# Block 2: v from stationary weights, then turned; pooled maps in attention steps 8 to 11; weight splits ahead of the sigmoids and by halves

## The reference, cut to what matters

```python
u = rms_norm_2(h, norm_mix[l])
proj = u @ w_in[l]
z_pool, q, k, v, g_pool, g_attn = jnp.split(proj, splits, axis=-1)
y_pool = multiscale_pool(z_pool, w_pool_group[l], pool_scale[l]) @ w_pool_branch[l]
y_attn = windowed_gqa(q, k, v, sink[l]) @ w_attn_branch[l]
merged = jax.nn.sigmoid(g_pool) * y_pool + jax.nn.sigmoid(g_attn) * y_attn
h = h + merged @ w_out[l]
u = rms_norm_2(h, norm_ffn[l])
h = h + (jax.nn.silu(u @ w_ffn_gate[l]) * (u @ w_ffn_up[l])) @ w_ffn_down[l]
```

## Time and profile before

| | us |
|---|---|
| median of 3 runs | 678.34 (677.67 to 678.72) |
| the profiled execution | 676.9 |
| span of its instructions | 675.1 |

### The profile page before, as it was taken

One profiled execution on the slowest core, in us unless ns is written; L12 is line 12 of the kernel. 1 busy time (PEld: TensorE's weight loads), 2 busy tenths in 40 slices (PEclk: granted clock), 3 DMA queues, 4 the chain that ended last, 5 costly groups with the idle time before them and its releaser, 6 DMA issues.

```text
span 675.1 us, 10135 instructions
## 1 busy us (share of the span) xinstructions
PE 628.7 (93%) x3987; PEld 470.5 (70%) x3987; DVE 359.2 (53%) x705; ACT 292.9 (43%) x553; POOL 49.4 (7%) x72
## 2 busy tenths in 40 slices
PE   8999999998998785879899999999999999999996
PEld 5979867743533230424389999898888888888884
DVE  5687765641031020110188977657866666666665
ACT  6855663321011010100185756655655555555554
POOL 2100102000010000000049000000100000000001
PEclk9999999999999977969999999999999999999998
DMA  8956429999999999999997334355545555555101
GB/s 340 419 237 250 179 105 405 371 399 425 426 386 426 420 420 423 419 421 422 422 420 276 132 125 148 106 185 188 186 164 190 201 190 192 187 187 187 63 1 62
DMA packets 26286, 180.73 MB, mean 268 GB/s; under 512 B 3184, under 2 KB 3312, under 8 KB 5120
## 3 DMA queue, kind: packets, MB, share of 16 engines
q1 hardware_dynamic: 25200, 177.60, 66.7%
q10 hardware_dynamic: 1040, 2.50, 1.0%
HBM read 179.04 MB, written 1.05 MB: 267 GB/s over the span
## 4 chain that ended last, share of the span: by engine, by line
PE 71%; DMA 14%; DVE 8%; ACT 4%; issue 2%; POOLq 0%; SPq 0%; POOL 0%; ACTq 0%; DVEq 0%
PE ps L1625 68%; DMA ring<-stream_dram 14%; PE ps L1628 3%; DVE ring_r L411 2%; ACT single L404 1%; DVE work L1560 1%; ACT work L900 1%; DVE work L1563 1%; DVE h L1613 0%; DVE work L1616 0%; ACT turned L905 0%; ACT work_r L896 0%; DVE extra_r L510 0%; DVE work L1441 0%; ACT work L810 0%
## 5 line engine op out<-in xcount | busy, mean ns | idle before, releaser
L1625 PE MATMUL ps<-turned,single 128*128 128x256 f32 (+2 forms) x944 | 231.5, 327 | 1.3 <-DVE turned L1578 0.6
L1625 PE MATMUL ps<-turned,ring_r 128*128 128x256 f32 (+1 forms) x648 | 179.7, 281 | 0.0
L1625 PEld LDWEIGHTS ps<-turned,single 128*128 128x128 f32 x944 | 156.4, 189 | 18.0 <-issue 2.0
L411 DVE TENSOR_TENSOR ring_r<-ring,single 128x1024 fp32r<-128x1024 f32 (+1 forms) x132 | 159.8, 1233 | 11.2 <-ACT single L404 11.0
L404 ACT ACTIVATE single<-ring 128x1024 fp32r<-128x1024 f32 (+1 forms) x132 | 134.1, 1047 | 0.1
L1625 PEld LDWEIGHTS ps<-turned,ring_r 128*128 128x128 f32 x648 | 121.1, 188 | 0.4
L1625 PE MATMUL ps<-ring,work 128*32 128x512 f32 (+2 forms) x462 | 71.0, 621 | 18.1 <-DMA ring<-stream_dram 15.8
L1625 PEld LDWEIGHTS ps<-single 128*128 128x128 f32 x257 | 38.3, 189 | 33.9 <-issue 20.5
L1625 PE MATMUL ps<-single,turned 128*128 128x512 f32 (+3 forms) x208 | 59.2, 364 | 1.6 <-DVE ring_r L411 0.9
L1625 PE MATMUL ps<-single 128*128 128x512 f32 (+1 forms) x257 | 55.3, 353 | 3.5 <-DVE single L1452 2.3
L1625 PE MATMUL ps<-single,work_r 128*128 128x512 f32 x176 | 56.2, 392 | 0.0
(11 more groups left out here) (260 smaller groups left out, 733.1 us busy)
## 6 DMA issues: line engine op xcount, KB each, us to landing
ring<-stream_dram SPq DMA_DIRECT2D x145, 1024.0 KB, 12.3
work<-stream_dram SPq DMA_DIRECT2D x12, 1024.0 KB, 11.4
turned_w<-stream_dram SPq DMA_DIRECT2D x4, 1024.0 KB, 14.0
extra<-stream_dram SPq DMA_DIRECT2D x2, 1024.0 KB, 12.0
ring<-stream_dram SPq DMA_DIRECT2D x2, 832.0 KB, 8.0
h<-x_dram SPq DMA_DIRECT2D x2, 512.0 KB, 5.0
gain<-gains_dram ACTq DMA_DIRECT2D x2, 512.0 KB, 11.0
yields<-stream_dram SPq DMA_DIRECT2D x1, 1024.0 KB, 12.4
```

Source lines behind the costliest of these rows:

```text
L411: dve.tensor_tensor(ring_r[:, place, a], ring[:, place, a], w_hi[k % HIGHS][:, a].bitcast(F32), ALU.subtract).then_inc(s["wlo_done"], 1)
L1625: return pe.matmul(o, lhsT, rhs, start=start, stop=stop, **kw)
```

## The change

- v becomes a chunk like the others (weights held, 256 tokens moving, into bank 1); ACT copies it to a spare buffer (`v2_turned`), and PE turns it back with two transposes in step 0, from where ACT scales it out as before, one step later. PE's 48 matmuls with 128 moving become 24 with 256 moving and two transposes.
- `values2` takes both token halves in one matmul: 4 matmuls with 256 moving (two runs of 128) instead of 8 with 128, and waits for all four turned probabilities at once.
- The pooled maps move into steps 8 to 11, one each, between scores and turning, into the free half of bank 4 or 5; ACT and DVE take them out in their loops. The turning of steps 10 to 13 waits for `yp_low` in addition.
- The branch phase no longer waits for `o2_low` at its start, but ahead of its second half of step 0.
- ACT's and DVE's splits move: slot 6 and 7 in the first steps; slot 15 ahead of the sigmoids; 16 to 20 one half for each step m.

```diff
+        def pool_map_place(c):
+            return ps[:, 4 + (POOL_MAPS_AT + c) % 2, TOK:2 * TOK]
...
+            act.wait_ge(s["v2_ps"], 1)
+            act.activation(v2_turned, ps[:, 1, 0:TOK], ACT.Copy).then_inc(s["v2_sb"], 1)
             def values_out():
-                act.wait_ge(s["v2_ps"], 1)
+                act.wait_ge(s["v2_ps"], 2)
...
+                if u == 2 * HEADS:
+                    split_high_half(act, SPLIT1 + 15, 0)
...
                 if u == 0:
+                    split_high(act, SPLIT1 + 6)
+                if u == 1:
                     values_out()
-                    split_high(act, SPLIT1 + 6)
-                if u < 2 * HEADS:
+                    split_high_half(act, SPLIT1 + 7, 0)
+                if POOL_MAPS_AT < u <= POOL_MAPS_AT + 4:
+                    pool_map_high(act, u - POOL_MAPS_AT - 1)
+                if 0 < u < 2 * HEADS:
                     split_high_half(act, SPLIT1 + 7 + u // 2, u % 2)
             attention2_out(act, CT - 1)
-            for m in range(4):
-                act.wait_ge(s["yp_ps"], m + 1)
-                act.activation(yp_hi[:, m, :], ps[:, (4, 5, 0, 1)[m], 0:TOK], ACT.Copy,
...
+            split_high_half(act, SPLIT1 + 15, 1)
             for m in range(DT):
                 act.wait_ge(s["g_sb"], m + 1)
                 act.activation(gate[:, m, :], gate[:, m, :], ACT.Sigmoid).then_inc(s["sig_done"], 1)
+            split_high_half(act, SPLIT1 + 16, 0)
             for m in range(DT):
-                if m % 2 == 0:
-                    split_high(act, SPLIT1 + 15 + m // 2)
                 act.wait_ge(s["mg_sum"], m + 1)
                 act.activation(mg_hi[:, m, :], gate[:, m, 0:TOK], ACT.Copy).then_inc(s["mg_high"], 1)
+                split_high_half(act, SPLIT1 + 16 + (m + 1) // 2, (m + 1) % 2)
...
-                if u:
+                if u == 2:
+                    split_low_half(dve, SPLIT1 + 7, 0)
+                if u > 1:
                     split_low_half(dve, SPLIT1 + 7 + (u - 1) // 2, (u - 1) % 2)
+                if POOL_MAPS_AT + 1 < u <= POOL_MAPS_AT + 5:
+                    pool_map_low(dve, u - POOL_MAPS_AT - 2)
...
+            split_low(dve, SPLIT1 + 15)
             for m in range(DT):
-                if m % 2 == 0:
-                    split_low(dve, SPLIT1 + 15 + m // 2)
...
+                split_low_half(dve, SPLIT1 + 16 + m // 2, m % 2)
                 dve.wait_ge(s["mg_high"], m + 1)
...
+            pe.wait_ge(s["z2_sb"], 3)
+            chunk(ps[:, 1, 0:TOK], SPLIT1 + 4, 1, (u_hi, u_lo)).then_inc(s["v2_ps"], 1)
...
+            def values_turned():
+                pe.wait_ge(s["v2_sb"], 1)
+                pe.wait_ge(s["q2_sb"], 3)
+                for i in range(NT):
+                    last = turn(ps[:, 6, i * P:(i + 1) * P], v2_turned[:, i * P:(i + 1) * P])
+                last.then_inc(s["v2_ps"], 1)
...
+                c = u - POOL_MAPS_AT
+                if 2 <= c < 6:
+                    pe.wait_ge(s["yp_low"], c - 1)
...
-            def values2(m, i):
+            def values2(m):
...
+                pe.wait_ge(s["pt2_sb"], 4 * (m + 1))
...
-                        last = mm(ps[j * HD:(j + 1) * HD, 6 + m % 2, i * P:(i + 1) * P], v2[:, k, kv * HD:(kv + 1) * HD],
+                        last = mm(ps[j * HD:(j + 1) * HD, 6 + m % 2, 0:TOK], v2[:, k, kv * HD:(kv + 1) * HD],
+                                  pt2[:, j:4:2, k * P:(k + 1) * P], k == 0, k == NT - 1, skip_group_check=True)
...
+                if POOL_MAPS_AT <= u < POOL_MAPS_AT + 4:
+                    c = u - POOL_MAPS_AT
+                    pe.wait_ge(s["dp_done"], c + 1)
+                    pe.wait_ge(s["pt2_sb"], u - 1)
+                    if c >= 2:
+                        pe.wait_ge(s["yp_low"], c - 1)
+                    mm(pool_map_place(c), vec[:, V_PG + c * P:V_PG + (c + 1) * P], dp[:, c, :], True, True
+                       ).then_inc(s["yp_ps"], 1)
+                if u == 0:
+                    values_turned()
...
             pe.wait_ge(s["yp_low"], 4)
-            pe.wait_ge(s["o2_low"], CT)
...
+                    if m == 0 and b:
+                        pe.wait_ge(s["o2_low"], CT)
```

More of the change, by code:

```diff
@@ L470, in attention2_out @@
         def attention2_out(act, hp):
-            act.wait_ge(s["o2_ps"], 2 * (hp + 1))
+            act.wait_ge(s["o2_ps"], hp + 1)
             act.activation(at_hi[:, hp, :], ps[:, 6 + hp % 2, 0:TOK], ACT.Copy).then_inc(s["o2_sb"], 1)
@@ L517, in gate_out, with pool_map_high, pool_map_low @@
                               row2.unsqueeze(1).to_broadcast([P, 2, TOK]), ALU.mult).then_inc(s["g_sb"], 1)
+        POOL_MAPS_AT = 8
+        def pool_map_place(c):
+            return ps[:, 4 + (POOL_MAPS_AT + c) % 2, TOK:2 * TOK]
+        def pool_map_high(act, c):
+            act.wait_ge(s["yp_ps"], c + 1)
+            act.activation(yp_hi[:, c, :], pool_map_place(c), ACT.Copy, scale=vec[:, V_PSC + c:V_PSC + c + 1]
+                           ).then_inc(s["yp_sb"], 1)
+        def pool_map_low(dve, c):
+            dve.wait_ge(s["yp_sb"], c + 1)
+            dve.scalar_tensor_tensor(yp_lo[:, c, :], pool_map_place(c), vec[:, V_PSC + c:V_PSC + c + 1],
+                                     yp_hi[:, c, :].bitcast(F32), ALU.mult, ALU.subtract).then_inc(s["yp_low"], 1)
         def turned_bank(t):
@@ L900, in _ @@
                 act.activation(gate[:, m, :], gate[:, m, :], ACT.Sigmoid).then_inc(s["sig_done"], 1)
+            split_high_half(act, SPLIT1 + 16, 0)
             for m in range(DT):
-                if m % 2 == 0:
-                    split_high(act, SPLIT1 + 15 + m // 2)
                 act.wait_ge(s["mg_sum"], m + 1)
                 act.activation(mg_hi[:, m, :], gate[:, m, 0:TOK], ACT.Copy).then_inc(s["mg_high"], 1)
-            for n in range(19, B2 + 2):
+                split_high_half(act, SPLIT1 + 16 + (m + 1) // 2, (m + 1) % 2)
+            split_high_half(act, SPLIT1 + 20, 1)
+            for n in range(21, B2 + 2):
                 split_high(act, SPLIT1 + n)
@@ L1567, in _ @@
                                   ).then_inc(s["mg_done"], 1)
-            for n in range(19, B2 + 2):
+            for n in range(20, B2 + 2):
                 split_low(dve, SPLIT1 + n)
@@ L2152, in _ @@
             chunk(ps[:, 0, 0:TOK], SPLIT1 + 4, 0, (u_hi, u_lo), frees=1).then_inc(s["k2_ps"], 1)
-            def values(i):
-                for t in range(DT):
-                    begin, last = triple(ps[:, 6, i * P:(i + 1) * P], [u[:, t, i * P:(i + 1) * P] for u in (u_hi, u_lo)],
-                                         [w[:, D + t * P:D + (t + 1) * P] for w in split_pair(SPLIT1 + 4)], t == 0, t == DT - 1)
-                return last
-            split_ready(SPLIT1 + 4, 1)
-            pe.wait_ge(s["q2_sb"], 3)
-            values(0)
+            pe.wait_ge(s["z2_sb"], 3)
[6 more added lines that the diff above has]
+                last.then_inc(s["v2_ps"], 1)
             def scores2(u):
@@ L2185, in turn_probs2 @@
                 last.then_inc(s["pt2_ps"], 1)
-            def values2(m, i):
-                u, kv = 4 * m + 2 * i, m // 2
-                pe.wait_ge(s["pt2_sb"], u + 2)
-                if u == 0:
-                    pe.wait_ge(s["v2_sb"], 1)
-                if m >= 2 and i == 0:
+            def values2(m):
+                kv = m // 2
+                pe.wait_ge(s["pt2_sb"], 4 * (m + 1))
+                if m == 0:
+                    pe.wait_ge(s["v2_sb"], 2)
+                if m >= 2:
                     pe.wait_ge(s["o2_low"], m - 1)
@@ L2196, in values2 @@
                     for j in range(2):
-                        last = mm(ps[j * HD:(j + 1) * HD, 6 + m % 2, i * P:(i + 1) * P], v2[:, k, kv * HD:(kv + 1) * HD],
-                                  pt2[:, 2 * i + j, k * P:(k + 1) * P], i == k == 0, i == 1 and k == NT - 1, skip_group_check=True)
+                        last = mm(ps[j * HD:(j + 1) * HD, 6 + m % 2, 0:TOK], v2[:, k, kv * HD:(kv + 1) * HD],
+                                  pt2[:, j:4:2, k * P:(k + 1) * P], k == 0, k == NT - 1, skip_group_check=True)
                 last.then_inc(s["o2_ps"], 1)
@@ L2204, in _ @@
             scores2(1)
-            values(1).then_inc(s["v2_ps"], 1)
             for u in range(2 * HEADS):
@@ L2214, in _ @@
                     scores2(u + 2)
+                if POOL_MAPS_AT <= u < POOL_MAPS_AT + 4:
[8 more added lines that the diff above has]
+                    values_turned()
                 if u and u % 4 == 0:
-                    values2(u // 4 - 1, 0)
-                    values2(u // 4 - 1, 1)
+                    values2(u // 4 - 1)
                 turn_probs2(u)
-            values2(CT - 1, 0)
-            values2(CT - 1, 1)
-            for c in range(4):
-                pe.wait_ge(s["dp_done"], c + 1)
-                if c == 2:
-                    pe.wait_ge(s["g_sb"], DT)
-                mm(ps[:, (4, 5, 0, 1)[c], 0:TOK], vec[:, V_PG + c * P:V_PG + (c + 1) * P], dp[:, c, :], True, True
```

(3 more changed lines are left out.)

7 lines of the change are left out of this document (1 added, 6 removed).

## The result

The changed kernel ran at a median of 674.61 us (674.12 to 674.76, four runs), the kernel before beside it at 678.53: a ratio of 0.9944 [0.9925, 0.9963], or 3.9 us. All three together, 26 runs of it against 77 of the kernel before, put the medians at 675.56 and 678.59 and the means at 675.98 and 678.51, so 2.5 to 3.0 us. Executions of one and the same kernel, before or after, differ by 4 us and more, and the experiments place nearly all of that difference ahead of the code that the change touches.

What follows compares the result with a forecast made beforehand. PE's matmuls were taken to bound the attention stretch; terms of -1.0 + 0 + 2.0 + 0.5 - 3.1 - 0.5 = -2.1 us, taken off the median of 678.34, gave 676.2 us, range 674.8 to 678.3.

Steps and rivals of the forecast that it cites:

- v: Start of the attention stretch: v made as a chunk saves 1.75 us, of which 1.0 us stays after step 2.
- the chain of distances: DVE's work up to step 2's probabilities, 7.41 us from 377.55, putting step 2's turning at 385.05 instead of 386.05.
- Values: Value matmuls in steps 4, 8, 12 and behind step 15: one wide matmul instead of two, no change in time.
- rival D: Value matmuls no longer run in pairs: 0.85 us more a call, 3.4 for four, total 679.6 us; chance 0.11.
- Last values: Behind step 15's turning: the last values now wait for all of ACT's copy, +0.5 us.
- The end: Between last values and branch: the 3.08 us of maps and waiting vanish, -3.1 us.
- the cover of 3 us behind the sigmoids: In the branch: DVE's second product is ready at 447.1, and PE asks for it at 450.1.
- The projection's wait: Output projection: PE's wait for a weight's low part before the matmul of 471.92 goes, -0.5 us.
- Rival E: The end is not freed, the branch waits for DVE behind the sigmoids: 678.3 us if it eats all; chance 0.04.
- maps: Steps 8 to 11: each pooled map adds 0.5 us to PE's loop, +2.0 us for four.
- Rival C: A map costs 0.7 instead of 0.5 us and DVE's chain in step 2 is 0.3 longer: 677.3 us; chance 0.20.

Runs made afterwards that it cites:

- splits back: The changed kernel with the branch's and projection's weight splits back in the old order; 141.43 us from the first block-2 matmuls to the feed-forward, in one execution.
- third profile of the changed kernel: The changed kernel measured once more with nothing changed; ratio 0.9952 to the kernel before, median 675.51 us, block 2 beginning at 344.53.

## Why the prediction was right, and where it was not

**What held.** PE's matmuls bound the stage, and the time came from where the prediction put it. v: -1.03 against -1.0, and for the reason given, PE standing at the turning of step 2 for DVE's low parts (0.47 us, where 0.6 was written, at 384.76, which is 385.02 on the clock of the kernel before; the chain of distances gave 385.05). Values: +0.04 against 0; the call takes 1.08 us against 1.09. The rule of the Trainium skill, "Advanced Engine Details and Errata", section "Memory Cachelines", that non-contiguous PSUM patterns slow matmuls, has no counterpart here on the reading side, and rival D with its 1.6 us a call falls by the same row. Last values: +0.53 against +0.5. The end: -3.19 against -3.1, and the cover of 3 us behind the sigmoids was there: the second product at 445.3 against a bound of 447.1. The projection's wait: -0.50 against -0.5 in this profile, -0.3 to -0.4 in the other two. Rival E, the branch waiting for DVE, did not happen, and would not have with the old order of splits either: in "splits back" the branch takes 22.99 us (435.83 to 458.82), and the price of 1.4 to 1.65 falls in the projection.

**The term that was mis-sized: maps.** 0.5 us each was taken between bounds of 0.43 and 0.65. A map adds 411.85 - 411.42 = 0.43: the lower bound, the bare stream time, and 1.69 in place of 2.0 for four. The "little for the weight load" was not there: PE's load for this map begins at 411.31, while the scores ahead of it still run. With that the sum is -2.4, and the stretch shows -2.20 to -2.55. Rival C (0.7 a map) falls.

**The step that failed: the runs' own spread, put at nothing on the low side of the range.** The sum of -2.1 was made within one profiled execution and taken off the median of three runs, 678.34, as if the next runs would be drawn alike. The low end of the range, 678.34 - 3.55 = 674.8, holds the favourable bounds of the kernel's terms and nothing for the runs; only the high end takes in 0.4 us, the distance of the three runs to their median. In place of that the runs show a spread of 4.65 us for the 77 of the kernel before, and a second profile of it that is 2.7 us longer, none of it behind 343. The first four runs of the changed kernel reached from 674.1 to 674.8, its next 22 from 674.0 to 678.8: the four were a lucky draw. The one of them that was profiled began block 2 at 343.01, the earliest of all twelve profiles; that the other three were early too is inferred from their times, not seen. The median of the kernel before beside them, 678.53, was an ordinary one. So of the 3.9 us, about 2.3 are the change, and 1.6 come from which executions, perhaps on which chip, the first four runs caught. The median of all 26 runs is 675.56, 0.6 below the forecast. Over all runs the medians still differ by 3.0 and the means by 2.5 us; whether what this has beyond 2.3 is chance or something ahead of block 2 is not shown.

**What stays open.** Why the first transposes take 1.97 us in one execution and 3.67 in another, with a granted clock of 1.00 in the records of both, is not shown; nor is what decides whether the clock falls near 148, or what else let the third profile of the changed kernel reach block 2 late. The Trainium skill, "TensorE: Matmul & The Clock Gate", section "Seeing it yourself", warns that the clock's own records can be unreliable, which would fit the first; no run here tells. Whether the 0.46 us at the first gate chunk can be had, by the low part of slot 5 ahead of q's, was not tried.

## What to carry to other kernels

Compare two versions between two fixed points of one execution around the change, and take the distance from a second profile of the unchanged kernel before trusting a median of a few runs: here the distance repeats within 0.3 us while the runs spread over 4. When an engine is let out of a gap, ask who was just in time because of the gap: with the old order of splits the maps were worth about 0.4 us, since ACT's and DVE's splits were as late as PE, and the new order without the maps about 0.7 (both estimates), while the two together gave 1.9. When a run is to be forecast, give its range the spread of the runs on both sides. A wait that a change leaves on the bounding engine is a place to put independent work: the fourth map cost 0.43 us in the loop and nothing in the wait.

## What the runs showed of the hardware

- A float32 pass of 256 columns between others of the same array shape adds no more than 0.43 us for the two passes of a map, with its weight load running under the matmuls before; eight passes of 256 on half the columns each take 1.08 us, as long as sixteen of 128 (1.09), though each reads two separate runs.
- One and the same program meets a different clock in different executions: 104 matmuls took 13.10 or 14.61 us around 146 to 162, with a granted clock of 1.00 or of 0.60 between 148 and 152.
- Where the weights' DMAs bound a stretch, a delay ahead of it is paid back in part: of 3.62 us, 0.97.
- A wait of the matmul engine costs more than the idle time in its row: 0.47 and 0.44 us of idle made two steps 0.64 and 0.61 us longer.
